# Filler products on TensorE at four places, and a new order for the first roundings, in a one-core mixer and expert-FFN kernel

## What is computed

```python
for l in range(DEPTH):                       # DEPTH = 1, 1024 tokens, D_MODEL = 1024
    h = rms_norm(x, g_mix[l]); proj = h @ w_in[l]
    y_pool = pool_mixer(u, w_pool[l], pool_scale[l])
    y_attn = forgetting_attention(to_heads(q), to_heads(k), to_heads(v), log_f)   # 8 heads of 64
    x = x + jnp.concatenate([y_pool, y_attn], axis=-1) @ w_out[l]
    h2 = rms_norm(x, g_ffn[l])
    x = x + moe_ffn(h2, w_router[l], b_router[l], w_up[l], b_up[l], w_down[l], b_down[l])
return rms_norm(x, g_final)
# moe_ffn: top 4 of 32 experts; per expert: clamped_swiglu(xb @ w_up[e] + b_up[e]) @ w_down[e] + b_down[e]
```

## Time and profile before

| | |
|---|---|
| median of three runs | 1937.5 us (1937.08 to 1940.15) |
| the profiled execution | 1945.72 us, span 1944.0 us |
| TensorE busy | 1876.1 us, 97% of the span |
| VectorE, ScalarE, GpSimd busy | 1177.5, 874.8, 251.6 us |
| mean granted clock of TensorE | 0.979 |
| weights rounded, first items | one piece: 1.92 us on ScalarE, 2.29 us on VectorE |

### The profile page before, as it was taken

How to read it: one execution, slowest core, us unless ns; L and a number is a source line. 1 busy time by engine, 2 the same in 40 slices (tenths; PEclk the granted TensorE clock), 3 DMA queues, 4 the chain that set the end, 5 groups by cost and what they waited for, 6 DMA issues and landing times.

```text
span 1944.0 us, 33770 instructions
## 1 busy us (share of the span) xinstructions
PE 1876.1 (97%) x12022; PEld 1595.9 (82%) x12022; DVE 1177.5 (61%) x1749; ACT 874.8 (45%) x1172; POOL 251.6 (13%) x212
## 2 busy tenths in 40 slices
PE   8999999999599999999999999999999999999995
PEld 6777788888488888888888788888888899898884
DVE  5343357622699999999999944444444344344446
ACT  4312345522576777777677633333333322232234
POOL 0000000000121222122122111111111111111100
PEclk9999979999699999999999999999999999999998
DMA  5223843233599999999999988887878887777773
GB/s 196 72 82 137 256 102 93 55 121 110 205 406 393 378 365 355 377 365 356 381 363 364 363 284 281 282 282 282 282 282 283 284 284 268 258 279 258 264 259 145
DMA packets 176239, 507.72 MB, mean 261 GB/s; under 512 B 13704, under 2 KB 14344, under 8 KB 159746
## 3 DMA queue, kind: packets, MB, share of 16 engines
q1 hardware_dynamic: 159074, 457.65, 64.1%
q0 software_dynamic: 16000, 47.31, 8.5%
q10 hardware_dynamic: 1120, 2.16, 0.3%
HBM read 469.29 MB, written 46.33 MB: 265 GB/s over the span
## 4 chain that ended last, share of the span: by engine, by line
PE 77%; DVE 2%; issue 1%; ACT 0%; DMA 0%; POOL 0%; DVEq 0%; ACTq 0%; PEldq 0%; POOLq 0%
PE ps L2081 26%; PE ps L2142 19%; PE ps L2223 6%; PE ps L2230 3%; PE ps L2117 3%; PE ps L2124 3%; PE ps L2091 3%; PE ps L2118 3%; PE ps L1974 2%; PE ps L1976 2%; PE ps L2063 2%; PE ps L1975 2%; PE ps L2205 1%; PE ps L2130 1%; DVE acc L1939 0%
## 5 line engine op out<-in xcount | busy, mean ns | idle before, releaser
L2081 PE MATMUL ps<-xg,weights 128*128 128x136 f32 (+2 forms) x4096 | 511.4, 287 | 2.6 <-DVE xg L1231 0.8
L2081 PEld LDWEIGHTS ps<-xg,weights 128*128 128x128 f32 x4096 | 505.1, 190 | 9.1 <-issue 9.1
L1827 DVE TENSOR_TENSOR weights_r<-weights,w_rounded 128x2048 fp32r<-128x2048 f32 x192 | 432.4, 2286 | 3.0 <-ACT w_rounded L1483 2.8
L1483 ACT ACTIVATE w_rounded<-weights 128x2048 fp32r<-128x2048 f32 x192 | 359.4, 1920 | 57.4 <-DVE weights_r L1827 27.2
L1357 POOL DMA_INDIRECT acc_d<-y_rows,row_index_now x62 | 111.8, 1802 | 803.5 <-ACT y_rows L1467 438.6
L1775 DVE TENSOR_TENSOR weights_r<-weights,w_down_rounded 128x1024 fp32r<-128x1024 f32 x128 | 148.1, 1219 | 28.4 <-PE ps L2095 28.4
L1333 POOL DMA_INDIRECT xg_rows<-h2g_d,row_index_next x64 | 107.3, 1676 | 339.8 <-DVE row_index_next L1758 205.6
L2142 PE MATMUL ps<-w_rounded,x_rounded 128*128 128x512 f32 x512 | 151.1, 397 | 0.0
L2142 PE MATMUL ps<-w_rounded,x_rest 128*128 128x512 f32 x512 | 148.8, 392 | 0.0
L1789 DVE TENSOR_SCALAR glu<-ps,b_up_t 128x136 f32<-128x136 f32 (+2 forms) x128 | 38.2, 361 | 178.0 <-PE ps L2081 178.0
L2142 PE MATMUL ps<-weights_r,x_rounded 128*128 128x512 f32 x512 | 129.9, 396 | 0.0
(11 more groups left out here) (314 smaller groups left out, 2954.6 us busy)
## 6 DMA issues: line engine op xcount, KB each, us to landing
weights<-in_w_up SPq DMA_DIRECT2D x128, 2048.0 KB, 10.4
weights<-in_w_down SPq DMA_DIRECT2D x64, 2048.0 KB, 11.8
weights<-in_w_in SPq DMA_DIRECT2D x3, 2048.0 KB, 8.5
xt<-in_x SPq DMA_DIRECT2D x8, 512.0 KB, 4.0
qk_d<-stage_rounded SPq DMA_DIRECT2D x16, 256.0 KB, 2.5
qk_d<-stage_rest SPq DMA_DIRECT2D x16, 256.0 KB, 3.0
q_stack<-qk_d SPq DMA_DIRECT2D x16, 256.0 KB
k_stack<-qk_d SPq DMA_DIRECT2D x16, 256.0 KB
```

What stands on the lines that cost most here:

```text
L1483: ins = act.activation(wh[SLOT[j]][:], src, ACT.Copy)
L1827: ins = dve.tensor_tensor(piece_of(raw_r, j)[1], piece_of(raw, j)[1], wh[SLOT[j]][:].bitcast(F32), ALU.subtract)
L2081: last = pe.matmul(o, raw[c][:, k, t * P:(t + 1) * P], xg[:, k, 0:w], start=(k == 0), stop=(k == KT - 1))
```

## The change

A helper `keep_busy(pe, bank, times)` issues `times` products of the bf16 identity with itself (512 columns, into one PSUM bank; nobody reads the result). It is called on TensorE at four places: ten products behind the projection's last group, ten behind attention's `y_inner`, 24 behind the first index product, eight behind the first item's transposes. For the first item TensorE adds 12 to `s_fr` before the index product and no longer behind the wait for the rows; and ScalarE spreads the bias column (`select_up(0)`) between pieces 0 and 1 and not behind both.

```diff
+        def keep_busy(pe, bank, times):
+            for _ in range(times):
+                pe.matmul(psum[bank][:].rearrange("p (a b) -> p a b", a=4), identb[:],
+                          identb[:].unsqueeze(1).to_broadcast([P, 4, P]), start=True, stop=True)
...
                     if half == 1 and n >= N_U + 5 and (n - N_U - 5) // 2 < NG:
                         pool_product((n - N_U - 5) // 2)
+                keep_busy(pe, 4, 10)
...
                 y_inner(NH // 2 - 1, TB // 2 * (NH // 2) + 1)
+                keep_busy(pe, 7, 10)
...
-                for j in range(AHEAD):
-                    round_piece(0, j)
+                round_piece(0, 0)
                 act.wait_ge(s_bt, 1)
                 select_up(0)
+                round_piece(0, 1)
                 x_narrow(0)
...
                 pe.sem_inc(s_ip, 1)
+                pe.sem_inc(s_fr, PIECES)
                 index_product(0, 1)
+                keep_busy(pe, 7, 24)
                 pe.wait_ge(s_tb, 1)
                 ends = class_ends(pe)
                 n_items = ends[-1]
                 pe.wait_ge(s_rw[0], 16)
                 pe.wait_ge(s_ix, 1)
-                pe.sem_inc(s_fr, PIECES)
                 x_narrow(0)
+                keep_busy(pe, 7, 8)
                 pe.wait_ge(s_bt, 1)
```

## The result

The changed kernel takes 1946.69 us (median of 9 runs, 1939.02 to 1947.86), the kernel before 1939.51 on the same chip (9 runs, 1937.08 to 1944.7): ratio 1.0028, interval 1.0015 to 1.004. By that ratio it is slower by some 5.4 us; ratio and interval are taken over all runs, and the two medians alone lie 7.2 us apart. The forecast, no change (1937.7 us, range 1933.8 to 1941.2, slower at a chance of 0.09), was wrong.

What follows compares the result with a forecast made beforehand. TensorE bounds nearly everything, at half speed in places, and the next wait behind each place decides. Terms 0 + 0.2 + 0 took the profiled 1945.72 to 1945.9 us, the median to 1937.7 us; range 1933.8 to 1941.2.

Steps and rivals of the forecast that it cites:

- carries over: Whole kernel: the runs' median, 8.2 us under the profiled time, was assumed to stay that far under after the change.
- place A: Projection into attention: up to 2.8 us net gained, then lost waiting for k near 255; net 0, bounds -2.8 and +0.5.
- the forecast's two prices: Ten fillers at full clock: 2.3 us from the profile's fp32r products, or 2.16 us by the Trainium skill.
- R3: Wait for k near 255 changes the half-clock stretch behind it: longer, +5, 1942.7 us, chance 0.06; shorter, -5, chance 0.05.
- Place B: Attention into output projection: fillers replace useful slow products, full clock from the start; +0.2 us, bounds +1.1 and -1.5.
- Place C: First item: TensorE 3.0 us ahead, all waited away before the down product at 552.51; net 0, bounds -3.0 and +2.1.
- The three new stops: First item: TensorE, ahead of its data, stops at 542.6, 548.5 and 551.5, in sum 3.5 us.
- Behind it TensorE has no wait: First item, behind the wait for `hidden_r` and the down product: no further TensorE wait for the rest of the item.
- R1: Landings at attention and first item not fixed, so the gains of 2.8 and 3.0 come through: 1931.9 us, chance 0.17.
- R2: First item: three close stops bring the clock down, 2.1 us lost; with the output projection's upper bound 1940.7 us; chance 0.11.
- R4: All filler places: fillers don't count for the clock, so only their time is left; 1940.6 us, chance 0.05.
- The bound on what can be told: Whole kernel: a measurement can tell from no change about 0.2%, 3.9 us.

Runs made afterwards that it cites:

- C alone: Kernel before with only the first-item edits (24 + 8 fillers, `s_fr` added earlier, bias column between the first roundings): 1941.05 us, ratio 1.001.
- A alone: Kernel before plus only the ten fillers behind the projection: 1945.74 us, ratio 1.0024.
- the filled wait: Changed kernel plus 16 fillers inside TensorE's first wait for the next heads' q and k, near 255 us: 1937.23 us, ratio 0.9988.
- B alone: Kernel before plus only the ten fillers behind attention: 1940.23 us, ratio 1.0003.
- the whole change with the earlier k: Changed kernel, with the second half of `w_out` loaded behind the third head's q and k: 1934.67 us, ratio 0.9977.
- the filled wait of the kernel before: Kernel before plus 12 fillers inside TensorE's wait for q and k near 255 us: 1936.67 us, ratio 0.999.
- all but A: Changed kernel without the ten fillers behind the projection: 1942.93 us, ratio 1.0021.
- the earlier k: Kernel before, with the second half of `w_out` loaded behind the third head's q and k, no fillers: 1935.43 us, ratio 0.9982.

## Why the prediction was wrong, and where it was right

**What bounds the kernel.** Right in kind: TensorE, its clock, and the next wait behind each place. Wrong in what the profile stood for. The forecast noted that the profiled time was 8.2 us above the median and took that as something that "carries over". It doesn't. An execution with the short stretch (C alone) needs 117.5 us from the wait's end to the last `y_outer`, before's profiled one 123.0: 5.5 of the 8.2 us are the long stretch. Another 0.7 lie behind it: in the profile of before the clock fell for 6.8 us around `y_inner`, in five of the seven profiles without B for 3.4 us only, and there the part up to the output projection's last group takes 114.0 us and not 114.7. **This is the step that failed:** place A's term, "the clock falls behind it as it does now. Net 0", read in an execution with the rare stretch and then carried over. The sum was made against an execution in which the loss was already paid, and then applied to a median in which it wasn't. In its place the runs show attention going from 151.5 to 157.7 us, and A alone with 8 of 12 executions in the slow group where the kernel before has 8 of 101.

**Place A.** The start of attention came out (+0.3 for +0.2) by two misses that cancel: the fillers took 0.17 us less than the 2.50 us worked out (they start 0.215 us apart and not 0.23, the lower of the forecast's two prices), and the barrier opened 0.75 us behind them and not 0.48. The clock was up at 222 to 229 in five of the six profiles with A; it was also up in two of the eight without. The landing of k came 33.9 us behind attention's first logits in the changed kernel, 34.0 in A alone and 34.7 in the filled wait, beside 34.0 to 34.8 in the six profiles without A that kept the loads; so it is tied to no progress of TensorE that would show above this scatter. The wait grew by 1.1 us and not by 2.8: TensorE reached it 2.0 us sooner behind the first logits, where 2.96 was the most (0.55 of the difference went into the wait for ScalarE at 225.93, the rest stays open), and the landing lay 0.9 us nearer. "The clock falls behind it as it does now. Net 0" holds against the profiled execution (157.7 us of attention beside 157.8) and fails against the usual one: from 151.5 to 157.7, +6.2. That is R3's direction, and its size (+5) was near, but by luck: R3 let a stretch of 20 us grow to 30, while the measured one grew from 20.5 to 23.9, and most of the loss is that it comes in most executions. Its chance (0.06) was far too small. I had asked by how much a 20 us stretch could grow, and not how often it comes.

**Place B.** Full clock from the first product, net +0.2 (114.88 beside 114.69) as forecast, though against a profile whose own stretch there was longer than usual. The bounds were too narrow on the bad side: in B alone the clock fell only as `y_inner` began (381.2), and from the last `y_outer` to the end of the output projection it was 116.2 us, +1.5. Over all profiles it is 113.2 to 116.2 with B and 114.0 to 114.7 without.

**Place C.** Rounding 0, which waited for chunk 0, the first bias product (11.9 us behind the index product for a forecast of 12.1, before 12.9), the clock over the pause and the down product at its old place (40.3 for 40.4) were as worked out. The three new stops were not quite: in sum 2.4 us and not 3.5, and none of them for `hidden_r`. The hidden rows came later than was held fixed (38.7 us behind the index product, before 37.9), and when TensorE was through with them `hidden_r` was there. "Behind it TensorE has no wait" was right for TensorE and still missed 0.2 to 0.4 us between it and the second next index product; the landing of chunk 4, which the forecast held fixed, came later.

**R1** is out for A and for C: neither gain came through. **R2** came in one of seven profiles with C, at 1 us and not 2.1. **R4** is out: fillers bring the clock back where it was down and hold it over a pause (back at 517.2 behind the first index product, before at 529.3; no fall at the filled wait of the changed kernel). They don't do so in each execution: 3.4 us at half clock came behind place A in the whole change with the earlier k, and 6.8 us behind the filled wait of the kernel before. **The bound on what can be told** was fair: the interval of after is 0.25% wide.

**What the runs show and what they don't.** Shown: place A alone is enough for the loss; filling the wait, shortening it or taking it out removes it; a kernel with a longer wait and no fillers is slower too. Not shown: that A is the only source, as the change less A still loses 0.21% and its first 380 us are the kernel before's. The long stretch is 13.65 us longer than the short one (20.5 less 6.8), which is 0.0035 of the mean clock over 1940 us, most of the 0.004 to 0.005 between the two groups of executions. That this stretch is what separates the groups is inferred from this sum and the profiles of related kernels; no fast execution of the kernel before was profiled. Not shown: why the stretch is 20 us in one execution and 7 in another behind nearly the same wait (2.44 and 2.52 us). In the profiles the clock fell anywhere from 1.4 us before to 1.7 us behind TensorE's return. The Trainium skill ("TensorE: Matmul & The Clock Gate", Part 1) says that the monitor runs free of the kernel, so that the same work meets it at another phase in each execution; the table agrees with that in kind, and no run here controls the phase. Nor is it shown why all but A was slower when B alone (1.0003) and C alone (1.001) were not measurably so, nor why A's fillers cost more than a wait lengthened as much without them (157.8 us of attention beside 154.4).

## What to carry to other kernels

When the profiled execution lies outside the runs' own range, find first which stretch makes it so, and forecast against the usual execution: a change can turn what one execution in twelve pays into what most pay. Time won ahead of a wait for a fixed landing isn't neutral on TensorE: the pause grows, and the clock may be paid for behind it, here some 6 us with fillers ahead of the pause and some 3 us in one profile with a pause made as long without them (attention of 157.7 and 154.4 us beside 151.5, the longer pause included). Fillers belong inside the pause that the clock falls behind, or the load that ends it belongs earlier. The second seems worth more: three kernels with the earlier k had 0.9977 to 0.9982, two with a filled wait 0.9988 and 0.9990, but the intervals overlap.

## What the runs showed of the hardware

The length of a half-clock stretch isn't set by the pause ahead of it alone. Behind pauses for k of 2.2 to 3.0 us it was 6.8, 13.65 or 20.5 us with the same instructions behind, and none in the one profile where the loads were in another order. With the pause at 3.7 us or more the clock was down before TensorE was back, in three profiles of three. Fillers at full clock start 0.215 us apart (ten take 2.33 us, 16 take 3.62). 24 of them, begun at half clock, took 6.87 us and ended where the full clock had been back for 3.7 us (517.2 to 520.9).
